# A two-model block kernel on one core: the order of ScalarE's copies in the seven-product units, and who adds up the first run's input

## The reference

```python
def swiglu(h, w_in, w_out):                      # first network
    a, b = jnp.split(h @ w_in, 2, axis=-1)
    return (jax.nn.silu(a) * b) @ w_out
...
f = jnp.square(jax.nn.relu(h @ mlp_w1[i])) @ mlp_w2[i]      # second network
```

## Time and profile before

| | |
|---|---|
| median of 3 runs | 2668.0 us (2667.74 to 2669.13) |
| the profiled execution's own time | 2670.47 us |
| its span | 2668.7 us |
| TensorE's clock over the span | 0.994 of full |
| busy: TensorE, VectorE, ScalarE, GpSimd | 97%, 52%, 45%, 40% |

### The profile page before, as it was taken

How to read it: one execution, slowest core, us unless ns; L and a number is a source line. 1 busy time by engine, 2 the same in 40 slices (tenths; PEclk the granted TensorE clock), 3 DMA queues, 4 the chain that set the end, 5 groups by cost and what they waited for, 6 DMA issues and landing times.

```text
span 2668.7 us, 40348 instructions
## 1 busy us (share of the span) xinstructions
PE 2582.0 (97%) x15940; PEld 2166.6 (81%) x15940; DVE 1395.2 (52%) x2479; ACT 1190.5 (45%) x2071; POOL 1069.3 (40%) x497
## 2 busy tenths in 40 slices
PE   8999999999999998999999999999999999999998
PEld 6887788887777777898987678889887778888987
DVE  4575543353533357253658857455445565644554
ACT  4454421222533344453543845344345774534543
POOL 2312233434322323464533634455542212554552
PEclk9999999999999999999999999999999999999999
DMA  8623244543222211223232022322331112232332
GB/s 325 230 96 122 83 157 150 182 175 107 75 87 72 72 64 48 92 99 95 92 99 95 17 75 91 95 88 95 111 103 60 44 48 72 87 103 83 100 96 86
DMA packets 49843, 271.62 MB, mean 102 GB/s; under 512 B 5583, under 2 KB 9319, under 8 KB 25608
## 3 DMA queue, kind: packets, MB, share of 16 engines
q1 hardware_dynamic: 45648, 265.71, 29.2%
q10 hardware_dynamic: 4024, 3.54, 0.6%
HBM read 267.09 MB, written 2.13 MB: 101 GB/s over the span
## 4 chain that ended last, share of the span: by engine, by line
PE 62%; issue 24%; DVE 7%; POOL 5%; ACT 3%; POOLq 0%; ACTq 0%; DVEq 0%
PE lin L869 13%; PE lin L871 13%; PE lin L870 13%; PE lin L1949 5%; POOL wlo L754 5%; PE lin L1951 5%; PE lin L1950 5%; DVE bank L3468 2%; PE lin L1421 2%; PE bank L1405 1%; DVE bank L3470 1%; PE bank L1439 1%; PE bank L1600 1%; DVE tlo L3496 1%; ACT ghi L2444 1%
## 5 line engine op out<-in xcount | busy, mean ns | idle before, releaser
L754 POOL TENSOR_TENSOR wlo<-raw,whi 128x1024 fp32r<-128x1024 f32 (+4 forms) x202 | 696.5, 3448 | 1317.5 <-ACT whi L2090 1317.5
L2090 ACT ACTIVATE whi<-raw 128x1024 fp32r<-128x1024 f32 (+4 forms) x202 | 295.4, 1462 | 605.0 <-PE lin L871 542.8
L869 PE MATMUL lin<-hhi,whi 128*128 128x512 f32 x1160 | 466.0, 402 | 6.5 <-issue 2.6
L871 PE MATMUL lin<-hhi,wlo 128*128 128x512 f32 x1160 | 453.7, 391 | 0.0
L870 PE MATMUL lin<-hlo,whi 128*128 128x512 f32 x1160 | 453.0, 391 | 0.0
L869 PE MATMUL lin<-ghi,whi 128*128 128x512 f32 x1136 | 446.5, 393 | 2.9 <-POOL wlo L754 2.1
L871 PE MATMUL lin<-ghi,wlo 128*128 128x512 f32 x1136 | 442.8, 390 | 0.0
L870 PE MATMUL lin<-glo,whi 128*128 128x512 f32 x1136 | 442.8, 390 | 0.0
L775 POOL TENSOR_TENSOR wlo<-raw,whi 128x512 fp32r<-128x512 f32 x200 | 265.1, 1338 | 213.4 <-ACT whi L2422 212.3
L869 PEld LDWEIGHTS lin<-hhi,whi 128*128 128x128 f32 x1160 | 218.6, 188 | 67.4 <-issue 14.9
L1949 PE MATMUL lin<-thi,whi 128*128 128x256 f32 x800 | 230.8, 289 | 33.9 <-ACT lin L2472 27.9
(11 more groups left out here) (537 smaller groups left out, 4408.9 us busy)
## 6 DMA issues: line engine op xcount, KB each, us to landing
raw<-in_w SPq DMA_DIRECT2D x139, 1024.0 KB, 4.9
raw<-in_w SPq DMA_DIRECT2D x85, 512.0 KB, 3.6
adw_a<-in_ada SPq DMA_DIRECT2D x30, 1024.0 KB, 5.0
adw_b<-in_ada SPq DMA_DIRECT2D x18, 1024.0 KB, 5.9
raw<-in_w SPq DMA_DIRECT2D x12, 768.0 KB, 5.5
raw<-in_w SPq DMA_DIRECT2D x8, 640.0 KB, 3.8
raw<-in_w SPq DMA_DIRECT2D x8, 384.0 KB, 3.0
x<-in_x SPq DMA_DIRECT2D x1, 2048.0 KB, 10.0
```

The lines of the kernel that those rows point to most:

```text
L754: nc.gpsimd.tensor_tensor(wlo[:, slot, 0:size], raw[:, slot, 0:size], whi[:, slot, 0:size].bitcast(F32), ALU.subtract).then_inc(s.wlo_ok, 1)
L869: pe.matmul(dst, lh, rh, start=first, stop=False)
L871: return pe.matmul(dst, ll, rh, start=False, stop=last)
L2090: act.activation(whi[:, slot, 0:size], raw[:, slot, 0:size], ACT.Copy).then_inc(s.whi_ok, 1)
```

## The change

On ScalarE, the high part of the next unit's first weight sum (`ahead(1)`) is issued after the copy of U to V instead of ahead of it. This holds in all 50 units; in the last unit of a run `ahead(1)` issues nothing.

For the first run of the ffn, GpSimd adds hi and lo of chunks 0 to 3 into `m` (`input_sums`), each as soon as that chunk is ready, between the lows of the last two of the single units. `FFN_H` is the count of `h_ok` there. VectorE waits for these four (`m_ok`), makes the first `tsum` of them, adds chunks 4 to 7, and goes on with the other sums. Its work behind them is in another order: `single(0)` and the first `tlo` go ahead of the first unit's three weight sums, and `single(1)` ahead of the low part of k = 2.

```diff
+FFN_H = 48
 ...
-       "hid_hi": 4, "t_sum": 4, "t_hi": 4, "t_ok": 4}
+       "hid_hi": 4, "t_sum": 4, "t_hi": 4, "t_ok": 4, "m_ok": 4}
@@ GpSimd
+            def input_sums(u):
+
+                for c in range(4):
+                    pool.wait_ge(s.h_ok, FFN_H + c + 1)
+                    nc.gpsimd.tensor_tensor(m[:, c, :], hhi[:, c, :].bitcast(F32), hlo[:, c, :].bitcast(F32), ALU.add)                        .then_inc(s.m_ok, 1)
+
             def all_lows(first, last):
 
                 u = first
                 while u < last:
+                    if u + 1 == SEVEN[0]:
+                        input_sums(u)
                     if u in ORDINAL:
                         seven_lows(u)
                         u += 1
                         continue
-                    v = u
-                    while v < last and v not in ORDINAL:
+                    v = u + 1
+                    while v < last and v not in ORDINAL and v + 1 != SEVEN[0]:
                         v += 1
                     lows(u, v)
                     u = v
@@ ScalarE, seven_run
                     act.activation(p5, Q[:, half0], ACT.Copy).then_inc(s.p5_ok, 1)
-                    ahead(1)
                     act.wait_ge(s.prod_mm, HAD["prod_mm"] + 7 * g + 3)
                     if u > u0:
                         act.wait_ge(s.y_ok, y0 + chunk0 + per * (u - u0))
                     act.activation(V[:, half0], U[:, half0], ACT.Copy).then_inc(s.seed_ok, 1)
-                    ahead(2)
+                    ahead(1, 2)
@@ VectorE
-            def combined_sums(stage, src):
+            def combined_sums(stage, src, other=None):
 ...
                 v.tensor_tensor(tsum[:, 0, :, :], quarter(0, half1), quarter(0, half0), ALU.subtract).then_inc(s.t_sum, 1)
+                if other is not None:
+                    other()
@@ VectorE, ffn_short
-                v.wait_ge(s.h_ok, n.at(s.h_ok))
-                chain(v.tensor_tensor(m[:, :, :], hhi[:, :, :].bitcast(F32), hlo[:, :, :].bitcast(F32), ALU.add))
-                combined_sums(0, m)
-                seven_sums(u)
+                def second_half():
+                    v.wait_ge(s.h_ok, n.at(s.h_ok))
+                    chain(v.tensor_tensor(m[:, 4:8, :], hhi[:, 4:8, :].bitcast(F32), hlo[:, 4:8, :].bitcast(F32), ALU.add))
+
+                v.wait_ge(s.m_ok, HAD["m_ok"] + 4)
+                combined_sums(0, m, second_half)
                 single(0)
                 combined_low(0, 0)
+                seven_sums(u)
                 combined_low(0, 1)
                 block_low(u, 1)
+                single(1)
                 block_low(u, 2)
-                single(1)
                 combined_low(0, 2)
                 combined_low(0, 3)
                 block_low(u, 5)
```

More of the change, by code:

```diff
@@ L578, in program @@
         s.t_ok = s.lf_mm
+        s.m_ok = s.lfh_ok
         s_raw = (s.raw0, s.raw1)
@@ L2026, in ffn_short @@
                 turned_y["ffn"] = n.at(s.y_ok)
+                assert n.at(s.h_ok) == FFN_H + DC, n.at(s.h_ok)
                 seven_run(4, 0)
```

## The result

The changed kernel takes 2632.6 us in the median of four runs (2629.4 to 2635.1), the one before 2668.05. The ratio is 0.9868, with a 95% interval of 0.9855 to 0.9881: 35.4 us faster, where 36 were forecast.

What follows compares the result with a forecast made beforehand. TensorE, busy 97% of the span, bounds the kernel. 2670.5 - 30.7 + 2.1 - 7.3 = 2634.6 us profiled, so the median is 2668.0 - 35.9 = 2632.1 us; range 2627 to 2637.

Steps and rivals of the forecast that it cites:

- The waits for the copy, -30.7: Fifth product of the units, held by ScalarE's U to V copy: 30 waits of 1.04 us go, -30.7 us.
- C22, +2.1: Seventh product in rectified units newly waits for VectorE's C22: 0.13 us in 16 units, +2.1 us, bounds 0 to +7.
- The first run, -7.3: First run's input sums: second product near 1047.4, seventh at about 1058.4; -7.3 us, bounds -4 and -9.5.
- The 1.0 us for the last single unit: TensorE waits about 1.0 us there for GpSimd's low, queued behind the adds; it costs nothing.
- A: Seventh product in 31 units or more: lows or C22 0.3 to 0.6 us later; 2638 to 2651; chance 0.16.
- B: First run: the input sums gain nothing, collisions with GpSimd or the clock take the 7 us; 2639; chance 0.05.
- C: Fifth product: another condition at the same time, so only the first unit gains; 2661; chance 0.03.
- D: Rectified units: GpSimd's lows 3 and 4 hold C22, seventh product 1.35 worse in 24 units; 2682; chance 0.02.

Runs made afterwards that it cites:

- the experiment that removes the wait: C22 issued ahead of the product of A on VectorE in the rectified units, on the changed kernel; the eight rectified runs were 1.75 us shorter.
- the first four experiments: Kernel before with ScalarE's order alone (2632.8 us), no collision (2632.8), both high parts ahead of the copy (2691.7); changed kernel with ScalarE's old order (2665.7).

## Why the prediction was right

**The waits for the copy, -30.7.** Right in place and number, and some 2 us too small. Of it, 28.7 lay behind the first run. The ten runs lost 28.75 with C22's new wait of 1.75 inside, so the copy's waits there were worth 30.5. The forecast counted each up to the product's first matmul; the second starts 0.19 us after it instead of 0.12, as in the rows of C22 above, and that comes on top 28 times. ScalarE's order alone took 34.4 us, and more work ahead of the copy made a wait 0.73 longer. Curing the slow sum and leaving the order took the same 34 us.

**C22, +2.1.** Right, down to the 16 units. 0.13 us in each was forecast; it is 0.08 in 14 of them and 0.36 in two, and the experiment that removes the wait gets 1.75 us back in the sum of the eight runs. In the changed kernel's list of waits nothing of it shows.

**The first run, -7.3.** The steps were right in kind and the size was off. By my own terms the first run should have ended 7.3 + 2 x 1.04 = 9.4 us sooner; by the measure it is 6.3. The second product starts 3.03 us into the run (forecast 2.6, from 1044.8 to 1047.4), the third 6.46 (5.9), the seventh 15.02 (13.6): 1.4 us late, because VectorE's list met GpSimd more often than the two times that I had counted:

```profile
1045.21 1.65 DVE L3054 TENSOR_TENSOR glo<-sq,ghi 128x512 fp32r<-128x512 f32 x1
...
1047.39 3.92 DVE L3508 TENSOR_TENSOR tlo<-tsum,thi 128x1024 fp32r<-128x1024 f32 x2
```

The 1.65 should be 0.69, the 3.92 should be 2.4, and the first weight sum took 1.79. GpSimd's four lows behind one another took 6.70 us there. Of the other 1.7 us, 1.5 are the low clock behind the seventh product (above), which I had left in the bounds. With -6.3 + 2.1 in its place the first run's own term would read -4.2, near the bound of -4. The term also mixed two causes: most of the gain in this run belongs to ScalarE's order, and the input part brought 1.2 us of it.

**The 1.0 us for the last single unit.** Right: TensorE waits there, for the low that now stands behind GpSimd's adds, and loses nothing, since the first product of the run starts without a wait.

```profile
1027.33 0.51 PE L879 MATMUL lin<-hhi,whi 128*128 128x512 f32 x1 [0.84 <-POOL wlo L756]
```

**The sum.** -35.9 forecast, -35.4 measured. The miss in the first run (3.1 us) is met by the copy's waits (1.8 more than forecast) and C22 (0.3 less); the stretches add up to -35.0. That the sum fits so well is partly luck: two misses ran against each other. The upper end of the range, 2637, was also tighter than its own terms allow: -30.7, +7 and -4 give 2640.

**The rivals.** A (0.3 to 0.6 us back in 31 units or more) didn't come: 0.36 in two units and 0.08 in 14. B (the input sums gain nothing) was closer than its chance of 0.05: they add about 1 us to ScalarE's order, and alone they can't be told from no change. Its price of 7 us was wrong, though, since ScalarE's order by itself gains 5.1 in the first run. C and D fell with the list of waits.

## What to carry to other kernels

An in-order engine that takes work ahead for the next round should first issue what the current round waits for. When a stall has two causes in series (a slow sum, and a copy queued behind it), compare the lateness with the cover: here 1.76 us late against 0.72 covered, so to take away 1.04 from either cause was enough, and the second cure brought only 1.9 (without the input sums) or 3.4 (with them) of its 34 us. Judge a new order of work by the end of the stage, not by one product's start: here it brought 0.66 us at the product and lost 0.83 at the end.

## What the runs showed of the hardware

A cast on VectorE, with one input in SBUF, was also held beside GpSimd's adds: 1.51 us at 1032.40, where the same cast takes 0.42 to 0.58 elsewhere. The Trainium skill's page "SBUF — State Buffer" (Who interferes with whom) names casts among the operations that can; I had counted only those with two inputs. The stretches at the low clock lie in part at other places in two executions of one kernel: the changed kernel's two traces share three and differ in one (near 440 us or near 25). The kernel before ran from 2660.2 us (mean granted clock 0.998) to 2670.5 (0.994) in 15 executions beside the first four experiments. A short wait of TensorE, here 0.08 us, shows as a longer first matmul and a late second, not as idle time, and even one of 0.36 us got no mark in its row.
